# Two memory products move from behind TensorE's expert branch to ahead of the jump that ends each of its arms

## The reference

```
for l in range(DEPTH):                       # DEPTH = 2
    ...
    x = layer_norm(DEEPNORM_ALPHA * x + mix, ln1_g[l], ln1_b[l])
    f = grouped_moe(x, w_router, router_bias, w_exp_gate[l], w_exp_up[l], w_exp_down[l])
    x = layer_norm(DEEPNORM_ALPHA * x + f, ln2_g[l], ln2_b[l])

def memory_attention(qm, mem, w_kv):
    kv = mem @ w_kv                          # does not depend on x
    ...
```

## Time and profile before

| | us |
|---|---|
| median of 3 executions | 2249.02 |
| lowest, highest | 2247.35, 2249.37 |
| the profiled execution, whole | 2250.36 |
| its span, first to last instruction | 2248.4 |
| TensorE busy in the span | 2200.8 (98%) |
| granted TensorE clock, mean | 0.997 |

### The profile page before, as it was taken

The page is one execution under the profiler, slowest core; times in us unless marked ns, Lnnn a source line. Parts: engine busy times, 40 slices in busy tenths (PEclk is TensorE's granted clock), DMA queues, the critical chain, the costliest instruction groups (busy, mean ns, idle before and its releaser), DMA issues.

```text
span 2248.4 us, 24692 instructions
## 1 busy us (share of the span) xinstructions
PE 2200.8 (98%) x9803; PEld 1392.6 (62%) x9803; DVE 1144.9 (51%) x1926; ACT 436.5 (19%) x988; POOL 3.1 (0%) x20
## 2 busy tenths in 40 slices
PE   9999999999999999999999999999999999999998
PEld 7755444544458765446444486788888888554453
DVE  3765775211137267763111237775456423587666
ACT  2001401211121014212111146420000002252110
POOL 0000000000000000000000000000000000000000
PEclk9999999999999999999999999999999999999999
DMA  8345934799983439436999912002222224403340
GB/s 351 146 183 219 384 139 172 296 398 427 428 366 121 179 150 409 190 150 231 394 427 427 420 46 113 1 1 98 90 75 82 78 103 166 189 10 150 140 178 19
DMA packets 45262, 457.93 MB, mean 204 GB/s; under 512 B 5416, under 2 KB 15706, under 8 KB 17498
## 3 DMA queue, kind: packets, MB, share of 16 engines
q1 hardware_dynamic: 35520, 449.85, 49.6%
q10 hardware_dynamic: 9626, 6.46, 0.9%
HBM read 455.15 MB, written 1.15 MB: 203 GB/s over the span
## 4 chain that ended last, share of the span: by engine, by line
PE 83%; DVE 7%; DMA 7%; DVEq 2%; issue 1%; ACT 1%; SPq 0%; POOLq 0%; POOL 0%; ACTq 0%
PE banks L603 80%; DMA ring<-in_w_exp_up 7%; PE banks L1714 1%; PE banks L759 1%; DVE ring L3030 1%; DVE tiny L3241 1%; DVE tiny L2579 1%; DVE arena L2593 0%; DVE arena L3256 0%; DVE ring L2324 0%; DVE arena L2298 0%; DVE banks L2576 0%; DVEq L2299 0%; PE banks L1190 0%; DVEq L2592 0%
## 5 line engine op out<-in xcount | busy, mean ns | idle before, releaser
L603 PE MATMUL banks<-ring,arena 128*64 128x512 f32 (+2 forms) x3302 | 960.7, 546 | 14.1 <-DMA ring<-in_w_exp_up 4.4
L603 PEld LDWEIGHTS banks<-ring,arena 128*128 128x128 f32 (+1 forms) x3302 | 449.5, 166 | 484.5 <-issue 449.9
L603 PE MATMUL banks<-arena 128*128 128x128 f32 (+7 forms) x1584 | 243.9, 344 | 3.7 <-issue 1.7
L603 PE MATMUL banks<-X,ring 128*128 128x256 f32 x1024 | 223.6, 380 | 0.5 <-DVE arena L2532 0.5
L603 PEld LDWEIGHTS banks<-X,ring 128*128 128x128 f32 x1024 | 195.0, 191 | 29.1 <-issue 2.3
L603 PEld LDWEIGHTS banks<-arena 128*128 128x128 f32 (+2 forms) x1584 | 155.3, 173 | 66.5 <-issue 34.4
L603 PE MATMUL banks<-arena,ring 128*128 128x256 f32 (+1 forms) x736 | 178.8, 399 | 0.1
L603 PEld LDWEIGHTS banks<-arena,ring 128*128 128x128 f32 x736 | 138.9, 190 | 36.7 <-issue 15.3
L2423 DVE TENSOR_TENSOR arena<-arena,banks 128x512 f32<-128x512 f32 x16 | 11.0, 687 | 278.7 <-ACT arena L1873 278.7
L603 PE MATMUL banks<-ring 128*128 128x256 f32 x616 | 137.0, 379 | 0.0
L603 PEld LDWEIGHTS banks<-ring 128*128 128x128 f32 x616 | 117.0, 190 | 15.9
(11 more groups left out here) (367 smaller groups left out, 1883.7 us busy)
## 6 DMA issues: line engine op xcount, KB each, us to landing
ring<-in_w_in SPq DMA_DIRECT2D x38, 2048.0 KB, 11.9
ring<-in_w_exp_up SPq DMA_DIRECT2D x32, 2048.0 KB, 16.4
ring<-in_w_exp_down SPq DMA_DIRECT2D x32, 2048.0 KB, 11.9
ring<-in_w_exp_gate SPq DMA_DIRECT2D x30, 2048.0 KB, 13.5
ring<-in_w_ada SPq DMA_DIRECT2D x24, 2048.0 KB, 11.0
ring<-in_w_ffn SPq DMA_DIRECT2D x22, 2048.0 KB, 7.7
ring<-in_w_out SPq DMA_DIRECT2D x8, 2048.0 KB, 13.1
ring<-in_w_down SPq DMA_DIRECT2D x8, 1408.0 KB, 5.9
```

Of the source, the lines that this page charges most:

```text
L603: ins = nc.tensor.matmul(out, weights, moving, start=start, stop=stop)
```

## The change

The first two products (in layer 1, the two context chunks) are written as `next_products()` and called inside both arms: in the first arm behind the scatter and ahead of the increment and the jump, in the second arm at its end. The transposes now follow the branch directly, and in layer 0 the third and fourth product follow them as before. The bookkeeping is set back for the second arm in two more places. Nothing else is edited, and the products, their order, their banks and their slots are the same.

```
-                begun = (dict(C.k), dict(last), unsent[0])
+                begun = (dict(C.k), dict(last), unsent[0], at[0], dict(turn))
                 with pe.If(more < 1):
                     last_scatter()
+                    next_products()
                     pe.sem_inc(o_used, PAIRS * N_OVER)
                 held = dict(last)
                 with pe.Else():
-                    C.k, unsent[0] = dict(begun[0]), begun[2]
+                    C.k, unsent[0], at[0] = dict(begun[0]), begun[2], begun[3]
+                    turn.update(begun[4])
...
+                    w = next_products()
-                last.clear()
-                last.update(held)
+                for b, read in held.items():
+                    last.setdefault(b, read)
                 settle(pe)
...
-                if l == DEPTH - 1:
-                    context_chunk(4)
-                    context_chunk(6)
-                    normed_rows_turned()
-                else:
-                    w = slot(next_tile(), DC, 512)
-                    for c in range(MEM_HEADS):
-                        if c == 2:
-                            normed_rows_turned()
+                normed_rows_turned()
+                if l < DEPTH - 1:
+                    for c in range(2, MEM_HEADS):
                         feature_product(w, c, memT, T, "act")
                     used()
```

```
+                def next_products():
+
+                    if l == DEPTH - 1:
+                        context_chunk(4)
+                        context_chunk(6)
+                        return None
+                    w = slot(next_tile(), DC, 512)
+                    for c in range(2):
+                        feature_product(w, c, memT, T, "act")
+                    return w
```

## The result

The changed kernel is slower: 2254.51 us against 2249.02 us, medians of 9 executions each, ratio 1.0028 with a 95% interval of 1.0020 to 1.0036.

What follows compares the result with a forecast made beforehand. TensorE, busy 98% of the span, was taken to bound the kernel; removing and reinserting the jump cost nothing, 2 x 0 = 0 us, so the forecast was the median, 2249.0 us, range 2247.0 to 2251.0.

Steps and rivals of the forecast that it cites:

- The two stall cases: At the moved jump, the longer jump leaves the loaded instructions: short stall 2250.0 us, chance 0.07; long stall 2263.6, chance 0.04.
- That moving the products gains nothing: Between last scatter product and products: taking the jump out returns nothing, at most 0.11 us a layer by the pace.
- Where the sequencer meets the jump: Behind the second product in layer 0: at about 651.0 us, having not lost the 0.75 us ahead of the products.
- the sign that was looked for in the weight loads: Behind the scatter: the weight load's 0.45 us of idle time should be gone from there.
- its sum is the same: Sequencer from scatter to transposes: 0.75 us saved ahead of the products, spent behind them, first transpose reached at 651.7 as before.
- The Trainium skill's rule: At the longer jump: 256-instruction blocks, sequential prefetch, a jump out of the current two waits; a stall if one more border is crossed.
- The short stall: Sequencer at the moved jump waits for one packet, resuming at 655.7, some 0.4 us late; 2250.0 us, chance 0.07.
- The long stall: At the moved jump, two packets in sequence hold the sequencer until 662.7, 7.3 us late a layer; 2263.6 us, chance 0.04.
- 4.5 us of cover: Between moved jump and transposes: a jump would have to take over 0.75 + 3.8 us before the array stood still.

Runs made afterwards that it cites:

- the run without a branch: Kernel before the change with TensorE's branch taken out, scatter and increment in the common stream, second arm left out: 2249.02 against 2249.45 us, ratio 0.9999.
- the shifted short arm: Changed kernel with the two products left out of the unrun second arm and 225 increments spread over the products of the first 160 us: 2250.12 us, ratio 1.0004.
- the shifted kernel: Changed kernel, both arms complete, with 155 semaphore increments spread ahead of the first branch, over the products of the first 160 us: 2254.05 us, ratio 1.0025.
- the shifted kernels: Two kernels with increments ahead of the branches: the changed kernel with 155 (2254.05 us), and it without the second arm's two products with 225 (2250.12 us).

## Why the prediction was wrong

The time, 2254.51 us, lies 3.5 us above the range of 2247.0 to 2251.0. The two stall cases had 0.11 of the chance, at 2250.0 and 2263.6; what happened lies between them.

**That moving the products gains nothing** was right: the run without a branch shows that the old jump was covered, and the shifted short arm that the products ahead of it don't make the kernel any faster.

**Where the sequencer meets the jump**, was put at 651.0, 3.3 us behind the last scatter product's start; it was 4.2 us behind it (651.10 - 646.94), 0.8 us later than forecast. The forecast had the sequencer win the 0.75 us that it lost at the old jump, and it doesn't: 4.0 us behind the scatter's last product it stands at the second product's end with and without a branch (the run without one, above), so what sets its place there is not the jump. For the same reason the sign that was looked for in the weight loads stayed out. The idle time of 0.45 us ahead of the first load didn't go, it came in two pieces:

```profile
647.48 0.19 PEld L603 LDWEIGHTS banks<-memT,ring 128*128 128x128 f32 x1 [0.24 <-issue]
647.91 0.62 PEld L603 LDWEIGHTS banks<-memT,ring 128*128 128x128 f32 x3 [0.24 <-issue]
```

The first load stands 0.54 us behind the scatter's first (646.94) and not 0.75, so the old jump delayed the loads by 0.21 us; the run without a branch has the same 0.54.

Right were the slots, the banks, the rows of the layer norm and the other engines: no new wait names one of them.

**The step that failed** is "its sum is the same", the exchange of 0.75 us ahead of the products for 0.75 us behind them. It took the jump at its old price. The jump had a new target, and the price hangs on the target's place: 6119 and 12310 lie beyond the borders at 6084 and (24 blocks on) about 12228, the old 5990 and 12117 ahead of them. (The count of places is a few off by layer 1: the stop of the shifted kernel came at place 12488 where 25 blocks behind 6084 are 12484. No case of layer 1 lies that close to a border.) The prediction counted how far the jump reaches, about 360 and 425, said that it matters where a border is crossed, and left the places uncounted and the case at 0.11 of the chance. They can be counted from the program before any run, with the border's offset, which I had no measure of, as the one unknown. In place of an exchange of equal costs the runs showed a jump of 6.70 and 6.09 us, and transposes that came 3.38 and 2.76 us late. The rows that it had, in which TensorE ran on behind the old jump, told only of the old target.

**The Trainium skill's rule** that spoke against the change ("Runtime: NRT & Kernel Launch", "Instruction fetch mechanics") was the right one: a taken jump beyond the two blocks waits for a fetch. The runs agree, with 6.0 to 6.7 us for ten such jumps and 0.3 to 0.4 us for eight into the next block; four others into the next block, of the shifted kernels, took 2.06 to 3.16 us, since that block was not yet in.

**The sizes.** The short stall was priced at 3.75 + 0.93 = 4.7 us, 0.4 us beyond the cover; it is 3.5 to 4.1 for the start, 0.9 to 1.2 for the packet and another 1.4 until the sequencer goes on, so 6.0 to 6.7. The long stall was to need two packets; one did it. The point from which it decides was put at 6.8 us of jump, with 4.5 us of cover; 6.70 and 6.09 were enough for 0.28%, since the cover was smaller. From the jump's start it was 3.7 us: the transposes were due at 646.94 + 7.87 = 654.81, and 6.70 us of jump and 0.4 us behind it, less 3.7, are the 3.4 us that they came late (658.19). The 3.38 and 2.76 us of both layers, 6.1 in all, pass the 4.5 us without the clock. The clock added 1.7 us in layer 0, which no term had, and gave back 1.6 us elsewhere. In the sum of the chances, 0.95 less 0.03 is 0.92 and not the 0.93 that stands there; nothing hangs on it.

## What to carry to other kernels

In these runs a jump over code that isn't run cost the sequencer 0.3 to 0.4 us while its target was in the block that was loaded next, and some 6 us when it was further, less what the array still had to do: count the instructions of the skipped arm, duplicates written into it included, and where it lands. Look also at the instructions right behind the target, since the block after it comes late: a border there stopped the engine for 1.1 to 4.7 us even when the jump was fast. Work in both arms of a branch lengthens the jump; work that can stand ahead of the whole branch doesn't.

## What the hardware showed that was not expected

- The next packet started only 3.5 to 4.2 us after a jump, fast or slow, in all 18 jumps but those of the two shifted kernels; so with a fast jump (0.41 us) and 6 instructions left in the block, TensorE stood still for 4.65 us.
- A jump soon after a border took 2.06 to 3.16 us, in four cases of two kernels: the target's packet started between 0.5 us before the jump and 0.8 us behind it, and the jump ended 1.4 us after it was in.
- The granted clock fell to 0.50 after 3.2 us of idle time in layer 0 of the changed kernel and stayed at 1.00 after 2.6 us in layer 1; when the changed kernel was run again it fell after 2.90 us in layer 0 and stayed at 1.00 after 2.89 us in layer 1, so the length of the idle time alone doesn't decide. It also fell to 0.50 with TensorE busy throughout, on products of 16 columns, in the kernel before, and in the changed one only behind the same products. Such stretches moved some 1.6 us from one place to another, so a part of the 5.3 us can't be told from this.
